# Encoder layer with expert-choice MoE: the finishing stage folded into the experts' second half, and the last expert split by group

## What is computed

```python
def expert_choice_moe(h, w_router, w_gate, w_up, w_down):
    ...
    gate, idx = lax.top_k(aff.T, cap)
    xe = xf[idx]
    hid = jax.nn.silu(jnp.einsum('ecd,edf->ecf', xe, w_gate)) * jnp.einsum('ecd,edf->ecf', xe, w_up)
    ye = jnp.einsum('ecf,efd->ecd', hid, w_down) * gate[..., None].astype(h.dtype)
    y = jnp.zeros_like(xf).at[idx.reshape(-1)].add(ye.reshape(-1, D))

    # in encoder_layer
    x = x + gate2 * rmsnorm(expert_choice_moe(h, ...), g_post_ffn)
```

## Time and profile before

| | us |
|---|---|
| median of three runs | 2589.13 |
| fastest and slowest run | 2586.8, 2592.96 |
| the profiled execution, its own time | 2585.97 |
| its span in the trace | 2584.2 |
| of it: `front` | 0 to about 1289 |
| `experts` | about 1289 to 2512 |
| `finish` | 2512 to 2584.2 |

### The profile page before, as it was taken

One profiled execution on the slowest core, in us unless ns is written; L12 is line 12 of the kernel. 1 busy time (PEld: TensorE's weight loads), 2 busy tenths in 40 slices (PEclk: granted clock), 3 DMA queues, 4 the chain that ended last, 5 costly groups with the idle time before them and its releaser, 6 DMA issues. The chain is left out here.

```text
span 2584.2 us, 35356 instructions
## 1 busy us (share of the span) xinstructions
PE 2305.1 (89%) x13449; PEld 1920.3 (74%) x13449; DVE 1200.7 (46%) x1847; ACT 1090.8 (42%) x1758; POOL 620.2 (24%) x615
## 2 busy tenths in 40 slices
PE   6999999999999978999606999999999999999940
PEld 4679889678898876677405888888888888888830
DVE  4212344544224346656493555555555545445416
ACT  4213444645434346655312444444444444444412
POOL 2003234233224234534311011111111111101003
PEclk9999999999999989999758999999999999999975
DMA  8635448456454477645345566666666666666529
GB/s 330 229 98 185 141 149 229 128 160 165 149 174 150 155 189 214 202 146 198 108 192 179 201 207 217 219 212 212 215 218 216 215 220 215 203 204 217 180 55 384
DMA packets 234890, 496.09 MB, mean 192 GB/s; under 512 B 36448, under 2 KB 127600, under 8 KB 231696
## 3 DMA queue, kind: packets, MB, share of 16 engines
q1 hardware_dynamic: 196528, 414.31, 47.6%
q0 software_dynamic: 35936, 71.75, 10.5%
q10 hardware_dynamic: 2304, 8.39, 0.8%
HBM read 405.40 MB, written 88.51 MB: 191 GB/s over the span
## 5 line engine op out<-in xcount | busy, mean ns | idle before, releaser
L2252 DVE TENSOR_TENSOR moe_w_lo<-moe_wf,moe_w_hi 128x2048 fp32r<-128x2048 f32 x192 | 439.9, 2292 | 550.7 <-ACT moe_w_hi L2174 550.7
L2174 ACT ACTIVATE moe_w_hi<-moe_wf 128x2048 fp32r<-128x2048 f32 x192 | 367.9, 1916 | 620.6 <-PE moe_acc L2305 602.1
L2305 PE MATMUL moe_acc<-moe_w_hi,moe_x_hi 128*128 128x512 f32 x1024 | 402.6, 393 | 6.9 <-ACT moe_hid L2188 5.5
L2305 PE MATMUL moe_acc<-moe_w_hi,moe_x_lo 128*128 128x512 f32 x1024 | 399.9, 390 | 0.0
L2305 PE MATMUL moe_acc<-moe_w_lo,moe_x_hi 128*128 128x512 f32 x1024 | 399.4, 390 | 0.0
L2305 PEld LDWEIGHTS moe_acc<-moe_w_hi,moe_x_hi 128*128 128x128 f32 x1024 | 192.9, 188 | 46.8 <-issue 6.0
L1732 PE MATMUL banks<-fr_w_hi,fr_h_hi 128*128 128x256 f32 x768 | 225.5, 294 | 0.0
L2305 PEld LDWEIGHTS moe_acc<-moe_w_hi,moe_x_lo 128*128 128x128 f32 x1024 | 192.8, 188 | 40.6
L2305 PEld LDWEIGHTS moe_acc<-moe_w_lo,moe_x_hi 128*128 128x128 f32 x1024 | 193.0, 189 | 39.3
L1732 PE MATMUL banks<-fr_w_lo,fr_h_hi 128*128 128x256 f32 x768 | 218.2, 284 | 0.0
L1732 PE MATMUL banks<-fr_w_hi,fr_h_lo 128*128 128x256 f32 x768 | 218.0, 284 | 0.0
(11 more groups left out here) (257 smaller groups left out, 4198.3 us busy)
## 6 DMA issues: line engine op xcount, KB each, us to landing
moe_wf<-in_w_expert_gate SPq DMA_DIRECT2D x64, 1024.0 KB, 4.9
moe_wf<-in_w_expert_up SPq DMA_DIRECT2D x64, 1024.0 KB, 4.8
moe_wf<-in_w_expert_down SPq DMA_DIRECT2D x64, 1024.0 KB, 5.1
fr_w_raw<-in_w_units SPq DMA_DIRECT2D x28, 1024.0 KB, 6.0
fr_bias<-in_na_bias SPq DMA_DIRECT2D x16, 1520.0 KB, 11.5
fr_a_w<-in_w_ada POOLq DMA_DIRECT2D x16, 1024.0 KB, 6.3
scratch_qk_t<-fr_stage SPq DMA_DIRECT2D x64, 256.0 KB, 2.5
scratch_vov<-fr_stage SPq DMA_DIRECT2D x96, 128.0 KB, 2.0
```

Source lines behind the costliest of these rows:

```text
L2174: nc.scalar.activation(w_hi[:, q, :, :], wf[:, q, :, :], ACT.Copy).then_inc(w_hi_ready, 1)
L2252: nc.vector.tensor_tensor(w_lo[:, q, :, :], wf[:, q, :, :], w_hi[:, q, :, :].bitcast(F32), ALU.subtract).then_inc(w_lo_ready, 1)
L2305: mm = nc.tensor.matmul(acc[:, j, b, :], x[:, g, k, :], w[:, q, a, h * HALF:(h + 1) * HALF], start=(k == 0 and i == 0), stop=(k == KC - 1 ...
```

## The change

The block `finish` is gone; its work is done inside `experts`.

- The loop covers experts 0 to 7. Experts 8 to 15 are written out. Where an expert is written out, the indirect DMAs take their index straight from `index_c`, without copy and drain. That holds too for the first two gathers, ahead of the loop.
- Both scatters of an expert wait for all scatters of the expert before, and no longer for each other: group 0 and group 1 are under way side by side.
- There are 26 *units* of result rows ahead of the last: 16 are whole tiles of 128 tokens, then 10 are the tokens of one expert in one group (experts 9 to 14), which are computed again since their `y` had grown after their tile was written. Four units run in each of experts 9 to 14, two in expert 15 (`window`). A unit is, all from POOL's queue: load `y`, load `x1` (plain for a tile, indirect for an expert's tokens), the power, and the store. ACT squares, DVE does the mean and the two operations of the result. They come in two pairs in an expert, with two buffers (`fy`, `fx`): the loads of a pair wait for the stores of the pair before. POOL takes the first pair once both scatters of the expert before have landed, and scatters the current expert's rows after the second pair's stores.
- The rows `gate2 * g_post_ffn` are made in expert 8.
- In the last expert PE runs group by group: UP for group 0 whole, half of UP for group 1, turn group 0, the rest of UP for group 1, half of DOWN for group 0, turn group 1, the rest of DOWN for group 0, DOWN for group 1. Nothing is scattered: POOL gathers `y` and `x1` of its tokens (`load_last`), DVE adds the products straight from PSUM (`add_last`), and the result goes out by an indirect store, for each group apart.

The diff, cut to its core:

```diff
+    FIRST, UNITS = 8, 4
+    units = [(t // TT, t, None) for t in range(GROUPS * TT)]
+    units += [(0, None, 9), (1, None, 11), (0, None, 10), (1, None, 12)]
+    units += [(0, None, 11), (1, None, 13), (0, None, 12), (0, None, 13)]
+    units += [(0, None, 14), (1, None, 14)]
...
-            with eng.Fori(0, NE // 2 - 1) as i:
+            with eng.Fori(0, FIRST // 2) as i:
                 for j in range(2):
                     body(i * 2 + j, j)
-            for j in range(2):
-                body(NE - 2 + j, j)
+            for e in range(FIRST, NE):
+                body(e, e % 2)
+
+        def window(e):
...
+            return range(UNITS * (e - FIRST - 1), min(LAST, UNITS * (e - FIRST))) if isinstance(e, int) and e > FIRST else range(0)
...
@@ gpsimd @@
-                nc.gpsimd.tensor_copy(idx_in[:, j, :], by_expert(index_c, e))
-                pool.drain()
+                if not isinstance(e, int):
+                    nc.gpsimd.tensor_copy(idx_in[:, j, :], by_expert(index_c, e))
+                    pool.drain()
...
             def body(e, j):
                 if not is_last(e, 2):
                     gather(e + 2, j)
-                scatter(e, j)
+                ns = window(e)
+                if ns:
...
+                    pool.wait_ge(added, (ZEROS + e * GROUPS) * 16)
+                    for half in (ns[0:2], ns[2:4]):
+                        for n in half:
+                            load_unit(n)
+                        if is_last(e) and half:
...
+                            for g in range(GROUPS):
+                                load_last(g)
+                        for n in half:
+                            root(n)
+                        for n in half:
+                            store_unit(n)
+                if not is_last(e):
+                    scatter(e, j)
...
+            def store_unit(n):
+                pool.wait_ge(out_ready, n + 1)
...
+                    pool.wait_ge(out_stored[j], 16 * (n // 2))
+                    if units[n - 1][0] == g:
+                        pool.wait_ge(out_stored[1 - j], 16 * ((n + 1) // 2))
...
@@ vector @@
+                    split(e, DOWN, range(0, 1))
+                    for n in ns[0:2]:
+                        mean(n)
+                    split(e, DOWN, range(1, 2))
+                    turned_out(e, h_hi, h_lo, j, h_hi_ready, h_ready)
+                    for n in ns[0:2]:
+                        result(n)
                     split(e, DOWN, range(2, NP))
+                    split(e + 1, UP, range(0, 2))
+                    for n in ns[2:4]:
+                        mean(n)
+                    for n in ns[2:4]:
+                        result(n)
+                    split(e + 1, UP, range(2, NP))
...
+            def add_last(g, j):
+                dve.wait_ge(last_loaded[0][g], 16)
+                for h in range(2):
+                    part = xe[:, g, h * HALF:(h + 1) * HALF]
+                    a = nc.vector.scalar_tensor_tensor(part, acc[:, j, 2 * g + h, :], gate_c[:, col(NE - 1, g)], part, ALU.mult, ALU.add)
+                a.then_inc(y_whole, 1)
...
@@ tensor @@
+                if is_last(e):
+                    bs = [range(2 * g, 2 * g + 2) for g in range(GROUPS)]
+                    products(e, UP, j, x_hi[:, j], x_lo[:, j], bs=bs[0])
+                    products(e, UP, j, x_hi[:, j], x_lo[:, j], first, bs[1])
+                    turn_h(e, j, bs[0])
+                    products(e, UP, j, x_hi[:, j], x_lo[:, j], second, bs[1])
...
+                    products(e, DOWN, j, h_hi, h_lo, first, bs[0])
+                    turn_h(e, j, bs[1])
+                    products(e, DOWN, j, h_hi, h_lo, second, bs[0])
...
+                    products(e, DOWN, j, h_hi, h_lo, bs=bs[1])
```

More of the change, by code:

```diff
@@ L2174, in split, with turned_out @@
                     nc.scalar.activation(w_hi[:, q, :, :], wf[:, q, :, :], ACT.Copy).then_inc(w_hi_ready, 1)
[L2176 to L2178 removed]
+            def turned_out(e, dst, turned, done, bs=range(BK)):
+                for b in bs:
                     act.wait_ge(turned, ONE + e * BK + b + 1)
```

311 lines of the change are left out of this document (176 added, 135 removed).

## The result

| | before | after |
|---|---|---|
| median | 2588.62 (4 runs) | 2506.59 (4 runs) |
| fastest and slowest run | 2586.8, 2592.96 | 2499.78, 2507.18 |
| the profiled execution, its span | 2584.2 | 2498.1 |

The changed kernel takes 0.9675 of the time before (95% interval 0.9654 to 0.9695, over all runs), 82.0 us less by the medians. The forecast was 2503.7, 2.9 us under the median; the time lies in the range.

What follows compares the result with a forecast made beforehand. TensorE was taken to bound the middle, loads and stores of `finish` the end. Savings 75.9 + 5.0 + 4.5 = 85.4 us (experts 9 to 14: 0) took 2589.1 to a median of 2503.7; range 2494 to 2522.

Steps and rivals of the forecast that it cites:

- 1. The tail: Behind the last product: 89.4 us without matmuls shrink to one group's chain and store, 13.5; saves 75.9 (73 to 78).
- 2. The last expert: Expert 15 by group: the other group's products fill TensorE's waits; 55.4 becomes 50.4 us, saving 5.0 (-2 to 10).
- The place in UP(15): Expert 15, splits for UP's third and fourth pieces, behind squares of units 22 and 23: 0 to 5 us of stall.
- that in DOWN(15): Expert 15, split of DOWN's fourth piece, behind late loads of units 24 and 25: 0 to 6 us of stall.
- 3. The start: First gathers of experts, without copy and drain, leave 4.4 us sooner and land about as much earlier; saves 4.5 (2 to 7).
- 4. Experts 9 to 14: Units hide beside TensorE's 69 us per expert, so they cost 0 us (bounds 0 to 10).
- 12 us of room: Experts 9 to 14: a w_lo split is ready three pieces less 4.2 us ahead, giving 12 us of slack.
- a rolling stall: Rival: units' loads land slowly in experts 9 to 14, TensorE stalls 3 to 6 us in each; 2522 to 2540, chance 0.09.
- near 1: By the skill page, an indirect DMA's issue beside a split would stay near 1 us, instead of the trace's 2.92.
- The third rival, VectorE held by GpSimd: VectorE waits while GpSimd issues, up to 3 us in experts 13 to 15 with indirect units; 2513, chance 0.03.
- The signs: Last 15 us one chain and store; t0 to last matmul 46 to 57 us; first turn 1364 to 1369; experts 69 apart.
- t0: Mark: start of ScalarE's split released by the last piece of DOWN(14), 2439.42 us in the profile before.

Runs made afterwards that it cites:

- squares behind: Changed kernel with squares and means of units 24 and 25 moved behind the work on group 1's turned hid in the last expert; 2503.07 us, ratio 0.967.
- the two slower kernels: Changed kernel with, per unit of experts 9 to 14, two more VectorE operations in one, a 1 MB DRAM copy in the other; 2539.4 and 2540.31 us.
- the start alone: Kernel before with one edit: the four gathers ahead of the loop take their index from index_c, without copy and drain; 2581.94 us, ratio 0.9975.

## Why the prediction was right, and where it was off

The total is nearer than its terms. The landing in the tail was forecast 3.2 us too long and its end 6.4 too short, and the start and the last expert gave 1.8 us more than forecast against 3.8 less from the tail. That these leave 1.9 us is luck.

**1. The tail, 13.5 forecast, 17.25 measured: the step that was mis-sized.** The chain down to the store's issue was forecast at 1.2 + 1.25 + 0.4 + 0.54 + 2.5 = 5.9 and took 6.4. The landing was taken from a scatter, 6.6, and was 3.4: a store that doesn't add lands sooner. The end of the block was taken at 1 us and took 7.4, of which 6.27 are the drain. It comes from a part of the change that I had costed at "under 1 us on an engine that is idle": without copies there are no drains from expert 8 on, and what each of them paid beside a landing is paid at the end. Before, GpSimd drained several times in each expert, and its last drain took 0.13 us; with one drain put back into each of the experts 9 to 14 it took 2.17. The saving was 72.1 instead of 75.9.

**2. The last expert, 50.4 forecast, 49.73 measured.** The sum was right in part by luck: I had taken 5 of 0 to 12, and its parts came out otherwise. The place in UP(15) cost nothing; that in DOWN(15) cost 2.55 us of wait, within 0 to 6, and 1.8 us of lower clock behind it, which no term of mine had. With both gone the expert took 45.3 (squares behind), against my 45.4.

**3. The start, 4.5 forecast, 5.65 measured** (5.6 alone). The earlier issue, 4.3 us, was as worked out; I had let the landing come earlier by just as much, and it gained 1.3 more. The rule of the Trainium skill (DMA: Bandwidth & Descriptors, Queues, rings and completion order) gave nearer 6, and the 5.6 us of the trace are nearer to that; that the rule is the reason isn't shown.

**4. Experts 9 to 14, 0 forecast, 0 measured** (962.09 us in both traces). The value was right, and the argument for it only in part. Busy time and slack of a split were right as numbers, but 5 us more per pair of units, on a path with "12 us of room", cost 7 to 13 us in experts with indirect units. I had named a rolling stall, by slow loads, and had left out how near it was: what counts is when the rows of a pair come round through its buffers to the square that stands ahead of a split, not the slack of the split alone. That the changed kernel lost nothing here doesn't show how near that was; the two slower kernels do.

The Trainium skill (SBUF — State Buffer, Who interferes with whom) infers that `tensor_tensor` does not hold up descriptors. That is again not borne out for indirect DMAs, while it fits plain ones. The rule that the same section states first, that such an operation and a GpSimd instruction exclude each other only where the latter reads SBUF, may fit both forms, since only the indirect one takes its indices from `index_c` in SBUF. My "near 1" had left that out; no run separates the two readings. Two issues of the changed kernel beside VectorE's work, an indirect and a plain one:

```profile
2411.67 2.78 POOL L2218 DMA_INDIRECT moe_fy<-scratch_y,moe_parts  x1 [0.30 <-issue]
```
```profile
2065.12 0.54 POOL L2214 DMA_DIRECT2D moe_fy<-scratch_y  x1 [0.19 <-issue]
```

The third rival, VectorE held by GpSimd, falls: the median of the splits is 2.29 us as before, the longest 2.38 (2.35 before).

**The signs** I had named came out: one chain and one indirect store in the last 17 us, 49.7 us between t0 and the last product with a single idle time ahead of DOWN's fourth piece, splits of 2.29 us, squares that wait 3.3 us at most up to the end of expert 14. The first turn, 1363.49, is under my 1364 to 1369 by the early end of `front`.

**The sum** was 85.4. By the marks the change gives 5.65 + 5.66 + 72.14 = 83.5, and the medians differ by 82.0. What is left is noise that the marks show: between kernels with the same `front` its end lies between 1289.63 and 1297.60, and from the first product to the fixed rhythm it takes either 100.7 to 101.2 or 102.7 to 103.2 us. The profiled run of the changed kernel had the early end and the fast start, so it lies 6.8 us under its own median, more than the 3.2 that I had added for that.

## What to carry to other kernels

Work that is hidden beside another engine's has two covers, the busy time and the chain through its buffers; follow the second one round before calling it free, and ask what a step would cost if it took twice as long. On an engine that runs in order, put an instruction that waits for a far DMA behind those that the bound engine wants next: four lines moved gave 4.4 us here. A drain on the queue that issues DMAs isn't free because nothing is under way, and taking drains out of a loop can move their price to the end, where nothing hides it.

## What the runs showed of the hardware

- With all of its DMAs landed, a drain on GpSimd took 0.13, 1.03, 2.17 and 6.27 us with 1, 12, 26 and 112 DMAs issued from its queue since the drain before, whether the last is plain or indirect, and 6.27 again when these 112 were spread over 34 us more. With 136, of which 24 are copies within DRAM, it took 3.98.
- The same wait of 6.78 us, followed by the same turn and the same matmuls, left TensorE at 2.4 GHz in one execution and at 1.2 GHz for nine matmuls in another, 2.3 us more. The start of `experts` takes one of two times, about 2.2 us apart; over the first 20 us from the first product the granted clock was 1.00 in the changed kernel (100.7 us) and 0.90 in the kernel with the start alone (103.0). So in these traces a gap cost up to 2.3 us more than its length.
- From GpSimd's queue a plain DMA of 512 KB is issued in 0.55 us beside VectorE's work, where an indirect load took up to 2.8 (0.94 with VectorE idle); an indirect store landed 3.4 us after its issue on idle DMA engines, an adding scatter 6.6.
